# Masked block products and the sixth output tile moved in among the block-inverse products

## The reference, cut to what matters

```python
def step(state, inp):
    r_t, w_t, k_t, v_t, kk_t, a_t = inp
    sa = jnp.einsum('bhvk,bhk->bhv', state, -kk_t)
    state = (state * w_t[:, :, None, :] + sa[..., None] * (kk_t * a_t)[:, :, None, :]
             + v_t[..., None] * k_t[:, :, None, :])
    return state, jnp.einsum('bhvk,bhk->bhv', state, r_t)
```

## Time and profile before

| | |
|---|---|
| median of 3 runs | 2302.39 us (2300.9 to 2304.96) |
| profiled execution | 2310.19 us, its span 2308.3 us |
| PE busy | 2270.2 us, 98% of the span |
| DVE, ACT, POOL busy | 1431.5, 1057.9, 267.4 us |
| mean granted TensorE clock | 0.992 |

### The profile page before, as it was taken

How to read it: one execution, slowest core, us unless ns; L and a number is a source line. 1 busy time by engine, 2 the same in 40 slices (tenths; PEclk the granted TensorE clock), 3 DMA queues, 4 the chain that set the end, 5 groups by cost and what they waited for, 6 DMA issues and landing times.

```text
span 2308.3 us, 35383 instructions
## 1 busy us (share of the span) xinstructions
PE 2270.2 (98%) x13166; PEld 1831.4 (79%) x13166; DVE 1431.5 (62%) x2068; ACT 1057.9 (46%) x1661; POOL 267.4 (12%) x201
## 2 busy tenths in 40 slices
PE   9999999999999999999999999999999999999998
PEld 7777877888887777867888887877888888888886
DVE  4678587666567678678666568676344357543443
ACT  5667355333246658345333247955233245432332
POOL 0042100000034032101000023210000012000002
PEclk9999899999999999899999999999999999999999
DMA  4210014556532210014555532222323221322322
GB/s 167 86 62 29 30 47 164 194 191 197 175 102 90 91 64 29 30 47 153 193 191 193 181 107 82 94 91 102 100 91 100 94 96 61 104 96 95 100 91 91
DMA packets 68799, 248.36 MB, mean 108 GB/s; under 512 B 7632, under 2 KB 8144, under 8 KB 68688
## 3 DMA queue, kind: packets, MB, share of 16 engines
q1 hardware_dynamic: 68688, 246.86, 32.1%
HBM read 244.73 MB, written 2.10 MB: 107 GB/s over the span
## 4 chain that ended last, share of the span: by engine, by line
PE 87%; DVE 6%; ACT 4%; issue 2%; DMA 1%; POOL 0%; SPq 0%; ACTq 0%; DVEq 0%
PE dense L698 24%; PE dense L700 23%; PE dense L699 23%; PE aux L698 2%; PE aux L699 2%; PE aux L700 2%; PE aux L1311 1%; ACT wh L1619 1%; PE aux L1101 1%; DVE wl L2544 1%; PE aux L1119 1%; PE aux L1222 1%; PE aux L1233 1%; PE aux L1089 1%; PE aux L1279 1%
## 5 line engine op out<-in xcount | busy, mean ns | idle before, releaser
L1619 ACT ACTIVATE wh<-raw 128x1024 fp32r<-128x1024 f32 x334 | 353.8, 1059 | 799.6 <-PE dense L700 789.3
L2544 DVE TENSOR_TENSOR wl<-raw,wh 128x1024 fp32r<-128x1024 f32 x334 | 415.4, 1244 | 377.7 <-ACT wh L1619 375.4
L698 PE MATMUL dense<-xh,wh 128*128 128x512 f32 x1600 | 633.8, 396 | 2.3 <-DVE xl L2579 1.2
L700 PE MATMUL dense<-xh,wl 128*128 128x512 f32 x1600 | 623.2, 389 | 0.0
L699 PE MATMUL dense<-xl,wh 128*128 128x512 f32 x1600 | 622.9, 389 | 0.0
L698 PE MATMUL dense<-hidh,wh 128*128 128x512 f32 x928 | 362.2, 390 | 1.1 <-ACT nt L2412 0.8
L698 PEld LDWEIGHTS dense<-xh,wh 128*128 128x128 f32 x1600 | 300.5, 188 | 77.8 <-issue 8.8
L699 PE MATMUL dense<-hidl,wh 128*128 128x512 f32 x928 | 361.1, 389 | 0.0
L700 PE MATMUL dense<-hidh,wl 128*128 128x512 f32 x928 | 361.1, 389 | 0.0
L699 PEld LDWEIGHTS dense<-xl,wh 128*128 128x128 f32 x1600 | 300.5, 188 | 63.5 <-issue 3.3
L700 PEld LDWEIGHTS dense<-xh,wl 128*128 128x128 f32 x1600 | 300.3, 188 | 63.1
(11 more groups left out here) (477 smaller groups left out, 2832.7 us busy)
## 6 DMA issues: line engine op xcount, KB each, us to landing
raw<-stream SPq DMA_DIRECT2D x362, 512.0 KB, 3.4
mraw<-mod_stream SPq DMA_DIRECT2D x96, 512.0 KB, 4.3
x<-x_t SPq DMA_DIRECT2D x4, 512.0 KB, 6.4
y_t<-x SPq DMA_DIRECT2D x8, 256.0 KB, 2.0
cst<-consts SPq DMA_DIRECT2D x1, 997.0 KB, 9.9
band<-bands SPq DMA_DIRECT2D x1, 576.0 KB, 4.4
cond<-c_rows SPq DMA_DIRECT2D x1, 512.0 KB, 10.9
pv_next<-vecs SPq DMA_DIRECT2D x3, 82.5 KB, 4.4
```

Of the source, the lines that this page charges most:

```text
L698: pe.matmul(o, a, h, start=first, stop=False, skip_group_check=placed)
L700: return pe.matmul(o, b, h, start=False, stop=last, skip_group_check=placed)
L1619: act.activation(wh[:, slot].rearrange("p k m -> p (k m)"), raw[:, slot, :], ACT.Copy).then_inc(hi_done, 1)
L2544: tt(wl[:, slot].rearrange("p k m -> p (k m)"), raw[:, slot, :], wh[:, slot].rearrange("p k m -> p (k m)").bitcast(F32), SUB)\
```

## The change

In both layers, and nowhere else:

- POOL masks `nT` after its wait for `xT32`, ahead of the masks of `bl` and `lkT`. Since `XT` is written at that time, `nT` lies elsewhere: in the place of `hats[:, 0]`, which the masked products' results fill, block after block.
- PE's masked products leave `prepare_chunks` and become `across(b)`, in the inverses; they use banks 0 and 1 in turn. ACT's four copies of them follow: that of block b comes after `pb(b + 1)`, the last after `pb(3)`. `prepare_chunks` ends at 32 banks.
- The output tile 5 of half 0 leaves the row of tiles and goes, one `mix_step` at a time, among the inverses' products.
- Ahead of the inverses' wait for `inv_turned`, PE makes four float32 products of 512 columns from constants into bank 0; nothing reads them.
- `solve` waits for the last copy of the masked products (`prep_read` 36).

```diff
-        rg = Region(vsb_at)
+        rg = Region(vsb_at + 4 * 4 * S)
-        nT = rg("nT", [P, 4, S])
+        nT = at("nT", [P, 4, S], front_at)
...
# PE, inverses
+                def across(b):
+                    pe.wait_ge(n_masked, L * 4 + b + 1)
+                    pe.wait_ge(prep_read, L * 36 + 30 + b + 1)
+                    for p in range(4):
+                        for e in range(2):
+                            for c in range(2):
...
+                    m.then_inc(prep_pe, 1)
-                pe.wait_ge(prep_read, L * 36 + 36)
+                pe.wait_ge(prep_read, L * 36 + 32)
+                for _ in range(4):
+                    pe.matmul(aux[0][:], const("ident"), cst[:, 0:S], start=True, stop=True)
                 pe.wait_ge(inv_turned, L * 2 + 2)
                 pe.wait_ge(cleared, 2 * L + 2)
                 product(0)
+                mix_begin(L, pl, 5, 0)
+                mix_step(L, pl, 5, 0, 0)
                 product(1)
+                across(0)
                 solved(0)
+                mix_step(L, pl, 5, 0, 1)
+                across(1)
                 product(2)
+                mix_step(L, pl, 5, 0, 2)
                 solved(1)
+                across(2)
                 product(3)
+                mix_step(L, pl, 5, 0, 3)
                 solved(2)
+                across(3)
                 solved(3)
...
# PE, the tiles ahead of the inverses (mix_begin of tile 1 waits for prep_read 32, not 36)
-                for m in range(6):
+                for m in range(5):
                     mix_out(L, pl, m, 0)
...
# ACT, after pb(b), b = 0 to 3
+                    if b:
+                        across(b - 1)
+                across(3)
...
# POOL
+                pool.wait_ge(prep_read, L * 36 + 16)
+                wait_apart(pool, inv_turned, L * 2 + 1)
                 for b in range(BLOCKS):
-                    pool.wait_ge(prep_read, L * 36 + 8 + 2 * b + 2)
                     masked(nT, b, "tri", n_masked)
-                wait_apart(pool, inv_turned, L * 2 + 1)
```

More of the change, by code:

```diff
@@ L1236, in prepare_chunks @@
                         i += 1
[L1237 to L1249, removed]
             def inverses(L, pl):
@@ L1267, in product @@
                     m.then_inc(p_pe, 1)
+                def across(b):
[4 more added lines that the diff above has]
+                            for c in range(2):
+                                r = HALVES[c]
+                                m = pe.matmul(aux[b % 2][r, p * P + e * HD:p * P + e * HD + HD],
+                                              nT[r, p, span(b, e)], hats[r, 4, p, span(b, e)],
+                                              start=True, stop=True)
+                    m.then_inc(prep_pe, 1)
                 def solved(b):
@@ L1301, in solve @@
                 pe.wait_ge(xt_ready, L * 2 + 2)
+                pe.wait_ge(prep_read, L * 36 + 36)
                 pe.wait_ge(u_read0, k)
@@ L2060, in prepare_chunks @@
                             i += 1
-                for dst in (hats[:, 4], hats[:, 1], bl[:, 0], hats[:, 3], hats[:, 0]):
+                for dst in (hats[:, 4], hats[:, 1], bl[:, 0], hats[:, 3]):
                     for b in range(BLOCKS):
-                        if i == 35:
+                        if i == 31:
                             act.wait_ge(bank_free[1], place1(L).bank(C_WO, 1))
@@ L2074, in scan_chunks, with across @@
                 halves = XT[:].rearrange("q p (n t) -> q (p n) t", t=HD)
+                def across(b):
+                    act.wait_ge(prep_pe, L * 36 + 32 + b + 1)
+                    act.activation(hats[:, 0, :, block_at(b)], heads(aux[b % 2][:]), ACT.Copy)\
+                       .then_inc(prep_read, 1)
                 def scaled_gate(p):
```

## The result

| kernel | median us | runs | least to greatest |
|---|---|---|---|
| before | 2305.56 | 20 | 2300.61 to 2308.14 |
| after | 2307.80 | 20 | 2303.82 to 2316.5 |

The ratio after / before is 1.0017, 95% interval 1.0009 to 1.0025. The time lies outside the forecast range. The two profiled executions alone say the opposite: 2310.19 before, 2305.35 after, a gain of 4.84.

A forecast was written before the change was run, and what follows sets the result against it. PE, busy 98%, was taken to bound the kernel, with a low-clock stretch in each layer. Saving 2.37 us a layer, 4.7 in all, gave 2302.4 - 4.7 = 2297.7 us, range 2295.2 to 2306.5.

The forecast's parts named there:

- I carry the difference over: Last step of the sum: the median lies 7.8 us below the profiled execution, so 2305.5 profiled becomes 2297.7.
- the release: DVE's last transpose, which lets the inverses start: moves from 245.24 to 243.00, 2.24 us earlier, in the first layer.
- My sum: PE's inverses at full clock: products, solved blocks, masked products and tile steps take 15.35 us against 12.00 today.
- the short fall: Rival, in the inverses: about 6 us at the lower clock cost 2.8 a layer, 2303.3 in all; chance 0.18.
- the long fall: Rival, in the inverses: clock falls as today for 17 us, costing 5.8 a layer, 2314 in all; chance 0.13.
- no two small products stand together any more: Argument against a falling clock: dense steps and masked products separate the inverses' 32-column products, except at the very end.
- DVE's three instructions: L2971, L2989 and the first L3016, slow beside POOL's masks, return to usual length: 0.88 + 0.54 + 0.82 = 2.24 us.
- The second solve: PE, behind the inverses: starts at 261.35, waiting for ACT's queued copy, later than DVE's way by 0.15.
- The scan: PE's products behind the second solve: start at 263.12 instead of 265.49, 2.37 us a layer earlier.
- the clock would need the dense steps beside the masked products: In the inverses: tile steps and masked products set among the small products keep the clock full throughout.
- most of the work that is moved pays back nothing: Balance: 3.35 us more in the inverses against 2.24 from DVE; the gain is some 7 us of lower-clock cost.

The follow-up runs named there:

- e11: The kernel before, unchanged, profiled once more: 2303.21 us, with 10.2 us at the lower clock in each layer.
- e8: The kernel before with four constant products spread among the inverses' products of each layer: 2304.26 us, ratio to before 0.9997.
- e5: The changed kernel with five constant products ahead of the inverses in place of four: 2305.19 us, ratio to before 0.9996.
- e10: The changed kernel, unaltered, in a third profiled execution: 2309.81 us.
- e2: The changed kernel with POOL's masks of nT back beside DVE's first steps: 2309.68 us, ratio to before 1.0029.
- e3: The changed kernel with the sixth output tile back ahead of the inverses, masked products and four constants kept: 2301.71 us, ratio to before 0.9986.
- e6: e3 with two constant products instead of four: 2300.78 us, ratio to before 0.9978.
- e7: e3 with three constant products instead of four: 2302.47 us, ratio to before 0.9987.
- e1: The changed kernel without the four constant products, so PE idles ahead of the inverses: 2322.8 us, ratio to before 1.0083.
- e12: e3 with one constant product instead of four, which leaves PE a wait of 0.7 us: 2299.96 us, ratio to before 0.9986.

## Why the prediction was wrong

**The step that failed: the profiled gain was carried over to the median.** I wrote that the median of the runs is 7.8 lower than the profiled execution, "and I carry the difference over". That treats 7.8 as an offset that belongs to profiling. It isn't: after's profiled execution, 2305.35, lies in the middle of its timed runs at full clock (2305.7). The 7.8 has two parts, and neither belongs to after:

- 4.6 is what the profiled execution of before, 2310.19, lies above the median of 20 runs, 2305.56. It lies above all 20; it ran 17 us a layer at the lower level where e11 ran 10, and its stretch is 113.75 - 108.92 = 4.8 longer. This part of the gain that I counted was already in the median.
- 3.2 is what the median of the three runs on which I built, 2302.39, lies below that of the 20. This made the forecast time too low and leaves the forecast gain as it is.

Against the forecast's 2297.7, after's full-clock executions stand at 2305.7: this step is worth 8.0 us, the 7.8 and 0.2 by which 2305.5 was too low.

The table says it in one line. The stretch takes 110.45 in after, 3.30 less than in the profiled before and 1.53 more than in e11. The usual execution lies between these two: of the 76 executions of before that were timed beside the experiments 14 have a mean clock of 0.992 or less, as the profiled one has, 26 have 0.993, 26 have 0.994, as e11 has, and 10 have more. For it the change saves some 10 us of lost clock (10.2 by e8's estimate) and pays 2305.7 - 2295.8 = 9.9 us of longer path. The rows give the same price: the inverses take 15.80 where products and solved blocks alone take 4.10 + 4.20 = 8.30 at the full clock, and the release comes 2.56 earlier, so 4.9 a layer. My sum had set 15.35 against today's 12.00, which holds the lower clock of that one execution.

**The second step that failed: the chance of the short fall.** I gave it 0.18 and the long one 0.13. I saw the wait (0.73 as measured; the constants took 3.60 of the 4.24 that I charged at most) and set against it that no two small products stand together any more. The wait was enough (e5): by their mean clocks 11 of 22 executions of after fell, seven for a short while, as in e10, and four for long. Those four, at 2314.9 to 2316.5, look like the long fall that I had priced at 2314, but none of them has a trace. e10, at 2309.8, is the short one; it cost 3.0 in the layer where it came, for a forecast 2.8, and its 2303.3 stood on the wrong base. The falls move the median from 2305.7 to 2307.8, 2.1 us. 8.0 + 2.1 are the 10.1 by which the forecast missed.

**What held.** DVE's three instructions came back to their usual length, by 2.2 at the forecast's rows. The release came 2.56 earlier after the first L1222 (37.20 before, 34.64 now; forecast 2.24), and e2 shows the cause. The inverses took 15.80 for a forecast 15.35: the four dense steps between small products take 0.90 each (243.93 to 244.83) where I had 0.79. The second solve is later than forecast by 0.6 and waits for ACT, as said. The scan came 1.5 and 1.8 a layer earlier than in the profiled before, for a forecast 2.37. Without the carry-over and at full clock the forecast of 2305.5 for the profiled execution was good to 0.2 us; that is in part luck: the two stretches gave back 3.3 of the 4.7, and the other 1.5 is the scatter of the rest.

**What I had argued wrongly without its costing anything.** That the clock would need the dense steps beside the masked products (e3: it doesn't). And "most of the work that is moved pays back nothing" was half of the truth: the tile among the products makes the path longer by 55.26 - 51.59 = 3.7 us a layer (e5 against e6, which also has three constants fewer), in a kernel that would have had its clock without it.

**What stays open.** Why executions of one program differ in where and for how long the clock falls (before: 10 or 17 us; after: none, 6.8, or long), what PE waits for in the scan, where the 4 us of scatter lie, and whether the 3 us that e6 and e7 lack belong to that. Whether ACT's queue, put in another order, gives back the 1.29 that the second solve waits in e6 wasn't tried.

## What to carry to other kernels

Before a gain read in one profiled execution is carried to the median, see where that execution lies among the timed runs and in their mean clocks; if it lies outside them, what made it slow may be the very thing the change removes, and only the part that a usual execution has can be won. Take the base from enough runs, too: three of them were 3.2 us off here. Where a clock that falls is the target, fill the wait ahead of the fragile stretch to its end: here 0.7 us of it left open went with a fall in half of the executions, and one more constant product cost nothing. Then take out what the clock doesn't need; here the sixth tile belonged ahead of DVE's release, where it was hidden.

## What the runs showed of the hardware

- The clock fell while PE was busy without a gap, 3.2 us into products of 32 columns, and held for 11.8 of 11.8 us when products of 64 columns stood among them (e6), and the mean clock was 0.998 or more in 33 of 33 executions of e3, e6 and e7.
- Behind a wait of 4.17 us the first product already ran at the lower level (e1); behind 2.22 us, dense products did for 3.4 us, though PE had been dense until then, and behind 2.19 us in the other layer none did (e2); behind 0.7 us the fall came in 11 of 22 executions of after, but in two of 12 timed ones of e12 for longer than 3.4 us, where no dense steps follow.
- The low stretch has no fixed length: 3.4, 6.8, 10.2, 13.7, 17 and 27 us were seen.
- Beside POOL's masks three DVE instructions took three to five times as long (1.29 for 0.43 us, 0.76 for 0.20, 1.04 for 0.22); a transpose of 128x1024 beside them took 2.04 us in after, and the one just ahead of it, beside no mask, 1.95.
- In the scan, identical work of PE took 44.2 to 47.0 us a layer, with stops of up to 1.27 us for which the profile shows no cause.
